# Nine projection parts of group A and B moved in front of the HGRN scan, modulation parts spread one by one

## The reference

```python
def reference(...):
    for l in range(DEPTH):
        mod_x = (s_c @ w_mod[l] + b_mod[l])[:, None, :]        # six blocks of 1024: shift, scale, gate, twice
        px = (h_x * (1.0 + ca_x) + sa_x) @ w_in[l]
        pc = (h_c * (1.0 + ca_c) + sa_c) @ w_in[l]
        mix_x, mix_c = _token_mixers(px, pc, ...)
        ...
def _token_mixers(px, pc, ...):
    (qa, ka, va, qb, kb, vb, qc, ic, fcf, fcb, gc, qd, kd, vd) = _split_cols(px)
    o_a = _window_attn_latent(_rope2d(_heads(qa), cos, sin), _rope2d(_heads(ka), cos, sin), ...)
    o_b = _global_attn_latent(_rope2d(nq(qb), cos, sin), _rope2d(nk(kb), cos, sin), ...)
    o_c, oc_ctx = _hgrn_mixer((qc, ic, fcf, fcb, gc), ...)
    o_d = _neigh_attn_latent(_heads(qd), _heads(kd), _heads(vd), ...)
```

## Time and profile before

| | us |
|---|---|
| three runs | 2174.01, 2171.15, 2176.42 (median 2174.01) |
| profiled execution | 2184.93 |
| its span on the core | 2183.1 |
| TensorE busy | 1991.6 (91%) |
| VectorE busy | 1400.0 (64%) |
| GpSimd busy | 998.0 (46%) |
| ScalarE busy | 823.7 (38%) |

### The profile page before, as it was taken

One profiled execution on the slowest core, in us unless ns is written; L12 is line 12 of the kernel. 1 busy time (PEld: TensorE's weight loads), 2 busy tenths in 40 slices (PEclk: granted clock), 3 DMA queues, 4 the chain that ended last, 5 costly groups with the idle time before them and its releaser, 6 DMA issues.

```text
span 2183.1 us, 32973 instructions
## 1 busy us (share of the span) xinstructions
PE 1991.6 (91%) x12812; PEld 1701.3 (78%) x12812; DVE 1400.0 (64%) x2711; ACT 823.7 (38%) x1584; POOL 998.0 (46%) x750
## 2 busy tenths in 40 slices
PE   6898988989998899999989998798898988999997
PEld 3678988867787788888878878697886776888786
DVE  3229988775586998999943362897877672222444
ACT  2233524346633222222243343342445633333442
POOL 1236755520154464333353334675624257655543
PEclk7998977999998889999999999887899999999999
DMA  7450100120021332333321121111030112222321
GB/s 319 174 193 21 40 21 20 40 112 2 21 78 39 116 116 100 130 118 116 116 78 68 49 97 59 39 40 39 21 131 2 40 58 77 97 97 97 116 87 68
DMA packets 26938, 177.31 MB, mean 81 GB/s; under 512 B 2720, under 2 KB 3744, under 8 KB 7712
## 3 DMA queue, kind: packets, MB, share of 16 engines
q1 hardware_dynamic: 22544, 157.90, 19.8%
q10 hardware_dynamic: 4240, 17.30, 2.0%
HBM read 171.00 MB, written 4.19 MB: 80 GB/s over the span
## 4 chain that ended last, share of the span: by engine, by line
PE 64%; DVE 16%; POOL 7%; issue 7%; ACT 3%; DMA 2%; DVEq 0%; SPq 0%; POOLq 0%; ACTq 0%
PE PS L1145 22%; PE PS L1070 17%; PE PS L830 5%; PE PS L836 4%; PE PS L1006 3%; PE PS L1031 3%; DVE W L1508 3%; PE PS L990 2%; PE PS L1126 1%; DVE W L1793 1%; DVE U L1694 1%; PE PS L921 1%; POOL WL L2087 1%; PE PS L996 1%; DVE W L1724 1%
## 5 line engine op out<-in xcount | busy, mean ns | idle before, releaser
L1145 PE MATMUL PS<-XH,WS 128*128 128x512 f32 x2016 | 551.8, 361 | 11.8 <-POOL WS L2128 10.8
L1145 PEld LDWEIGHTS PS<-XH,WS 128*128 128x128 f32 x2016 | 365.4, 192 | 69.7 <-POOL WS L2128 7.6
L1145 PE MATMUL PS<-XL,WS 128*128 128x512 f32 x1008 | 362.4, 359 | 0.0
L2128 POOL TENSOR_TENSOR WS<-WR,WS 128x1024 fp32r<-128x1024 f32 x88 | 213.9, 2434 | 321.0 <-ACT WS L1363 320.7
L1432 ACT ACTIVATE W<-PS,PR 128x768 f32<-128x768 f32 (+1 forms) x88 | 78.0, 886 | 451.3 <-PE PS L1145 389.1
L1985 DVE SCALAR_TENSOR_TENSOR W<-PS,PR,W 128x511 f32<-128x511 f32 (+1 forms) x132 | 83.0, 656 | 215.0 <-ACT W L1432 215.0
L1145 PEld LDWEIGHTS PS<-XL,WS 128*128 128x128 f32 x1008 | 194.0, 192 | 27.6
L1508 DVE SCALAR_TENSOR_TENSOR W<-WR,SC,W 128x256 f32<-128x256 f32 x336 | 201.4, 641 | 6.0
L836 PE MATMUL PS<-EU,XH 128*128 128x256 f32 x624 | 194.9, 312 | 6.9 <-issue 6.3
L2087 POOL TENSOR_TENSOR WL<-WR,EU 128x512 fp32r<-128x512 f32 x96 | 126.5, 1339 | 140.7 <-ACT EU L1205 140.6
L836 PE MATMUL PS<-WL,XH 128*128 128x256 f32 x624 | 190.4, 305 | 0.0
(11 more groups left out here) (218 smaller groups left out, 4482.7 us busy)
## 6 DMA issues: line engine op xcount, KB each, us to landing
WR<-in_weights SPq DMA_DIRECT2D x134, 1024.0 KB, 4.8
U<-in_weights SPq DMA_DIRECT2D x10, 1024.0 KB, 6.9
U<-in_bias ACTq DMA_DIRECT2D x2, 1792.0 KB, 10.2
H<-in_x SPq DMA_DIRECT2D x1, 2048.0 KB, 10.7
H<-in_x ACTq DMA_DIRECT2D x1, 2048.0 KB, 15.2
U<-in_ln_rows ACTq DMA_DIRECT2D x2, 1024.0 KB, 4.3
WR<-in_weights SPq DMA_DIRECT2D x4, 512.0 KB, 3.6
kept<-H ACTq DMA_DIRECT2D x4, 512.0 KB, 2.6
```

The source lines that it names most:

```text
L1145: mm = pe.matmul(PS[u.pos][:, lo:hi], w[:, part, k, :], src[:, k, lo:hi], start=(k == 0 and src is xh3 and part == 0), stop=(k == KT - 1 a ...
L2128: pool.tensor_tensor(ws5[:, u.c % 2, 1], half_slot(u), ws5[:, u.c % 2, 0], ALU.subtract).then_inc(w_low, 1)
```

## The change

ORDER becomes QC, GC, IC, QB, KVB, KVA, FCF, FCB, QA, VD, QD, KD, and own holds everything in front of FCF. So the parts of QB, KVB and KVA (nine in layer 0, eight in layer 1) leave the scan and stand in front of it, and the parts left beside the scan (QA, VD, QD, KD) are spread over the same 22 steps from step 3 on. In layer 0 eight of these steps (3, 5, 8, 11, 14, 16, 19, 22) have no part; in layer 1 eleven have none (3, 5, 7, 9, 11, 13, 15, 17, 19, 21, 23), where before it was three (3, 10, 17). The 16 modulation parts of layer 0 come one behind each projection part instead of mostly two. The fourth place for modulation weights moves within U. `project` on VectorE and the low pieces on GpSimd take the rotations and the roots along.

```diff
-ORDER = (QC, GC, IC, FCF, FCB, QA, KVA, QB, KVB, VD, QD, KD)
+ORDER = (QC, GC, IC, QB, KVB, KVA, FCF, FCB, QA, VD, QD, KD)
+OWN = ORDER.index(FCF)
...
-    own = whole(QC) + whole(GC) + whole(IC)
+    own = [p for s in ORDER[:OWN] for p in whole(s)]
...
-    rest = [p for s in ORDER[5:] for p in whole(s)]
+    rest = [p for s in ORDER[OWN + 2:] for p in whole(s)]
...
-    for at in range(4):
+    for at in range(OWN + 1):
         opening = [n for n in starts if own[n][0][2] == ORDER[at]][0] + (at == 0)
         behind[opening] = at + 1
-    for at in range(5, len(ORDER)):
+    for at in range(OWN + 2, len(ORDER)):
...
-        places = [WR[:, r * SLOT:(r + 1) * SLOT] for r in range(RING)] + [U[:, 17920:17920 + SLOT]]
+        places = [WR[:, r * SLOT:(r + 1) * SLOT] for r in range(RING)] + [U[:, 3072:3072 + SLOT]]
...
                     if j.is_e:
                         forget(j)
+                    if j.rope:
+                        rotate(j)
...
-                for n in sorted(splits[l][0]):
-                    for q in range(PIECES):
-                        low_weights(l, splits[l][0][n], q)
+                for n, j in enumerate(own_of[l]):
+                    if n in splits[l][0]:
+                        for q in range(PIECES):
+                            low_weights(l, splits[l][0][n], q)
+                    head_roots([j] if j.kind != "mod" else [])
```

## The result

| | us |
|---|---|
| before, median of 4 runs | 2173.17 (2171.15 to 2176.42) |
| changed, median of 4 runs | 2194.60 (2193.58 to 2200.86) |
| ratio | 1.0103, 95% interval 1.0080 to 1.0126 |
| profiled execution, span | 2194.51, 2192.7 |

The change makes the kernel 21 us slower, where 31 were forecast. The page of the changed kernel: busy time of each engine, and the granted clock in 40 slices, to be laid beside the earlier trace rows.

The account below looks back on a forecast made before the run. Bound: a chain through several engines beside QB and KVB (GpSimd's roots waiting for VectorE), elsewhere TensorE. Layer 0 +52 - 45 = +7, layer 1 +55 - 31 = +24, together +31 us, giving 2205 from 2174.01; range 2147 to 2228.

Parts of the forecast that it names:

- the front: Ahead of each scan: the moved parts and their turns add net 52 us in layer 0, 55 in layer 1.
- the rotation wait in layer 1's front: Layer 1's front: TensorE waits for QB and KVB rotations, charged 5 us, bounds 0 and 12, clock fall included.
- The walk: Layer 1's front, timed through: QB rotations end near 13 and 22, KVB's first near 29; TensorE wants the last at 25 to 26.
- the parts behind empty steps: Both scans: every part behind an empty step is charged 4.95 us for a clock fall, seven times in layer 0, nine in layer 1.
- empty steps: Scan steps without a part: eight in layer 0 at 5.96 us each, 47.7 in all.
- steps 11 to 15 of layer 1: Layer 1's scan, empty, VD, empty, QD, empty: 33 us, with empty steps at 5.96 then 4.66, parts at 10 and 8.
- The tail: End of layer 1's scan: a context feature part leaves it, about 3 us saved.
- the reading of the bound: Steps beside QB and KVB: 6.83 us of issue on GpSimd, 2.02 of roots, only then the scan's gates and keys.
- The faster rival: Both scans: clock stays up despite empty steps, the 4.95 charges fall away; -18 to -25 us, 2149 to 2156; chance 0.27.
- VectorE's bound: Faster rival's scans: with the clock up, VectorE and GpSimd limit the steps, layer 0 to 170 us, layer 1 to 142.
- Its price of a step without low pieces: Faster rival, both scans: such a step takes 7.5 us at least on average, 9.3 where low pieces are made.

Follow-up runs that it names:

- the filled steps: Changed kernel plus 20 useless TensorE products in each empty scan step that has a part behind it (nineteen steps); 2172.84 us, ratio 0.9990 against the kernel before.
- their control: Changed kernel plus the same 20 useless products, placed behind the empty step right ahead of its part; 2231.51 us, ratio 1.0270 against the kernel before.
- the packed kernel: Changed kernel with scan parts one per step from step 3 on, empty steps together at the end; 2182.75 us, ratio 1.0036 against the kernel before.

## Why the prediction was right, and where its sizes were off

In sum layer 0 came to -2.3 where +7 was forecast, and layer 1 to +21 where +24 was. The kernels with one layer changed bear this split out (no change that can be told, and +15).

*Right: the front is paid in full.* Forecast +52 and +55, measured +50.5 and +56.6. TensorE's idle time in layer 0's front is nearly gone: one wait for a rotation of 1.04 us is left, and none for weights.

*Right in size, misplaced: the rotation wait in layer 1's front.* Charged with 5 us (0 to 12), it is 5.66, and then the clock is down for some 2 us more. But it is the second QB part that TensorE waits for, not KVB's. TensorE, GpSimd, then VectorE (idle in brackets):

```profile
1371.12 1.11 PE L900 MATMUL PS<-CN,U 128*128 128x128 f32 x4 [5.66 <-DVE U L1670]
```

```profile
1360.92 1.98 POOL L2029 TENSOR_TENSOR ST<-ST,SC 128x4 f32<-128x4 f32 x2 [5.91 <-DVE ST L1628]
1362.87 5.51 POOL L2092 TENSOR_TENSOR WL<-WR,EU 128x512 fp32r<-128x512 f32 x4
```

```profile
1355.05 0.76 DVE L1633 TENSOR_TENSOR U<-U,ST 128x256 f32<-128x256 f32 x2 [5.69 <-POOL ST L2029]
...
1362.94 2.93 DVE L1633 TENSOR_TENSOR U<-U,ST 128x256 f32<-128x256 f32 x2 [2.09 <-POOL ST L2029]
1365.90 2.77 DVE L1641 TENSOR_TENSOR U<-U,PR 128x256 f32<-128x256 f32 x2
```

The walk forgot KVA's low pieces: they start as soon as the second roots are done, and VectorE's next two pairs take 2.93 and 2.77 us instead of 0.76, which is 4.2 of the 5.66.

*Right: the parts behind empty steps are charged.* Fifteen of the sixteen ran at 0.62 to 0.75, and the sum of the parts behind empty steps in layer 0 is 90.6 us, where 56.9 + 27.5 + 11.1 = 95.5 was forecast. Why it was right is shown by the filled steps and their control, as far as the filler kept the clock up. The rule of the Trainium skill (TensorE: Matmul & The Clock Gate, "HAM oscillation — how this bites in real kernels"), that a loop with waits between its bursts of products can start every turn at the lower clock, is borne out here in fifteen of sixteen turns.

*Too high: empty steps.* At 5.96 they were priced by the one behind a busy VectorE; the eight of layer 0 took 43.3 us in all where 47.7 was charged. The largest single miss is steps 11 to 15 of layer 1, 25.4 us where 33 was written. Steps 12 to 15 have no maps, and the empty ones among them were still priced at 4.66, the length of a step with maps. Steps 13, 14 and 15, each from its turn of the keys on:

```profile
1535.62:1536.24 0.62, 0.62 (x5) 0.43 (x5) 0.29 (x1) 0.52 (x2) 0.10 (x1) 1.00 0.00 0
1536.24:1542.88 6.64, 6.18 (x29) 4.79 (x29) 5.82 (x18) 4.69 (x13) 3.51 (x6) 1.00 0.45 158
1542.88:1545.56 2.68, 0.69 (x5) 0.43 (x4) 0.86 (x4) 2.65 (x9) 2.68 (x3) 1.00 0.01 3
```

The three empty steps (11, 13, 15) took 2.97 + 0.62 + 2.68 = 6.3 us where 15.3 was charged; the two parts (12 and 14) took 12.5 and 6.6 where 10 and 8 was, together about right, one at 0.73 and one at full clock. With 2.8 less for the first feature part behind them this is the 10 us by which layer 1's scan was better than forecast. The tail went the other way: a part in it stands at half clock, +2.6 for -3.

*Wrong: the reading of the bound.* The chain's 6.83 us of issue at the roots was told as a wait of GpSimd that holds up the gate. Taking the gate out from behind it changed the steps by 0.3 us each (the keys still stood behind it). The roots did cost, 3.5 us a step, but the steps are filled by VectorE's instructions and its own wait for the roots, and not by GpSimd's wait. The sum didn't rest on it, since it took a step with such a part and a step without as they stood.

*The faster rival* gave 79 us back for a clock that stays up and stopped at VectorE's bound, 170 and 142 us for the two scans, 2149 to 2156 in all. It did not come about, since the clock fell. How good its times were is open: with the filler the scans measured 176.6 and 154.9 and the time 2172.84, but 68 us at the lower clock were left, and filling costs about 1 us a step (5.69 for 4.69 in the one shown). Its price of a step without low pieces (7.5 us) looks like the packed kernel's 7.3 to 7.5, but those steps ran at half clock with TensorE busy 6.3 us of each, and most filled empty steps of the changed kernel took 5.4 to 6.0 at full clock; that agreement is luck. What is shown is that with half of the time at the lower clock gone, this change only comes out even.

## What to carry to other kernels

Ask for each piece of work that you move what it had been covering, and what it had been covered by: here products beside a chain on VectorE were free, and in front of it they cost every microsecond. What hurts in such a scan is work on the engine that is behind (here norms and rotations), so that is what to move or split, without the products that it belongs to. And keep TensorE's parts close together: a part with a sparse step ahead of it ran at 0.62 to 0.75 of full speed, and even 2.4 us of useless products in each such step were worth 22 us in all, while in a row of empty steps at the end of the scan they gave nothing.

## What the runs showed of the hardware

- Two fp32 additions or products of VectorE over 128x256, both operands in SBUF, take 0.76 us alone and 2.93 beside GpSimd's low pieces of 1.38 us each. Each of the two took 1.50 us for 0.42, so it lost 1.08 us, near the length of one GpSimd instruction. This agrees with the Trainium skill (SBUF — State Buffer, "SBUF: two separate sides"), by which the two engines lock a shared pair of ports for a whole instruction.
- Ahead of the fall to 1.2 GHz at 382.13 us TensorE had worked through the maps, turns and outputs of one step, waited 1.31 us, and worked through the maps and turns of the next; then it was idle for another 2.79 us. The fall lasted 6.83 us there and 10.24 us in other steps.
- Not settled: why the stretch between layer 0's attention and layer 1 takes 846 to 849 us in some executions and 852 to 853 in others. It was seen with and without the change.
